# One more wait ahead of the experts' first weight loads into the ring, in a two-layer hybrid trunk with a routed mixture of experts

## What is computed

```python
def moe(h, router_w, router_bias, w_gate, w_up, w_down):      # 16 experts, width 1024 -> 256 -> 1024
    ...
        scores = jax.nn.sigmoid((xb @ router_w).astype(jnp.float32))
        sel = scores + router_bias
        ...
        # best group of 4 experts by its two best, then the top 2 experts inside it
        combine = jnp.sum(jax.nn.one_hot(e_idx, N_EXPERTS, dtype=jnp.float32) * wts[..., None], 1)
        hid = jax.nn.silu(jnp.einsum('td,edf->tef', xb, w_gate)) * jnp.einsum('td,edf->tef', xb, w_up)
        return jnp.einsum('tef,te,efd->td', hid, combine.astype(hid.dtype), w_down)
```

## Time and profile before

| what | value |
|---|---|
| median of the runs | 1359.54 us |
| the profiled execution | 1359.39 us |
| its span, first to last instruction | 1357.6 us |
| PE, DVE, ACT, POOL busy | 75%, 39%, 21%, 6% |
| DMA: all data, mean rate | 239.50 MB, 176 GB/s |
| mean granted TensorE clock | 0.849 |

### The profile page before, as it was taken

The page is one execution under the profiler, slowest core; times in us unless marked ns, Lnnn a source line. Parts: engine busy times, 40 slices in busy tenths (PEclk is TensorE's granted clock), DMA queues, the critical chain, the costliest instruction groups (busy, mean ns, idle before and its releaser), DMA issues. The chain is left out here.

```text
span 1357.6 us, 23829 instructions
## 1 busy us (share of the span) xinstructions
PE 1021.0 (75%) x10191; PEld 703.7 (52%) x10191; DVE 532.0 (39%) x1335; ACT 286.3 (21%) x610; POOL 85.6 (6%) x144
## 2 busy tenths in 40 slices
PE   4999768399758888875499967849857975987651
PEld 3556556388435675532355646539734564553321
DVE  0255462956562331111415554486574142111103
ACT  1210344322410211100121044432240030110000
POOL 0000000000000012211100000000000002221111
PEclk8999868789978868999699977769977967998775
DMA  9596313400116179997732231240014119999933
GB/s 387 208 261 213 125 63 125 186 5 8 63 54 260 62 281 359 357 380 256 261 114 94 96 122 63 88 162 4 8 63 170 51 38 388 329 363 371 378 102 140
DMA packets 39443, 239.50 MB, mean 176 GB/s; under 512 B 5344, under 2 KB 5344, under 8 KB 15776
## 3 DMA queue, kind: packets, MB, share of 16 engines
q1 hardware_dynamic: 26784, 194.56, 38.2%
q0 software_dynamic: 12544, 43.27, 10.1%
HBM read 210.02 MB, written 27.79 MB: 175 GB/s over the span
## 5 line engine op out<-in xcount | busy, mean ns | idle before, releaser
L836 PE MATMUL bank<-sb_hT,sb_ring 128*128 128x385 f32 (+1 forms) x640 | 211.0, 490 | 5.0 <-ACT sb_hT L1378 5.0
L836 PE MATMUL bank<-sb_arena 64*64 64x64 f32 (+6 forms) x1184 | 139.6, 326 | 42.9 <-DVE sb_arena L1630 24.0
L836 PEld LDWEIGHTS bank<-sb_hT,sb_ring 128*128 128x128 f32 (+1 forms) x640 | 119.2, 188 | 93.8 <-issue 12.3
L1378 ACT ACTIVATE sb_arena<-bank 128x384 f32<-128x384 f32 (+5 forms) x166 | 69.9, 442 | 368.3 <-PE bank L836 266.5
L836 PEld LDWEIGHTS bank<-sb_arena 128*64 128x64 f32 (+2 forms) x1184 | 87.4, 150 | 74.1 <-DVE sb_arena L1630 25.3
L839 PE MATMUL bank<-sb_consts,sb_arena 64*128 64x64 f32 (+1 forms) x451 | 62.9, 289 | 57.4 <-DMA sb_arena<-x_slots 28.7
L1378 ACT ACTIVATE sb_u<-bank 128x256 f32<-128x256 f32 (+2 forms) x92 | 41.7, 463 | 261.3 <-PE bank L836 260.6
L836 PE MATMUL bank<-sb_ring,sb_arena 128*64 128x256 f32 (+1 forms) x536 | 86.4, 474 | 11.4 <-DMA sb_ring<-weights 8.3
L836 PE MATMUL bank<-sb_o,sb_ring 128*128 128x385 f32 x256 | 86.9, 502 | 9.5 <-issue 9.5
L839 PEld LDWEIGHTS bank<-sb_consts,sb_arena 64*128 64x128 f32 (+1 forms) x451 | 50.4, 165 | 80.4 <-issue 76.2
L1630 DVE TENSOR_TENSOR sb_arena<-sb_arena,bank 128x128 f32<-128x128 f32 (+1 forms) x91 | 26.0, 320 | 162.6 <-ACT sb_arena L1378 148.2
(11 more groups left out here) (174 smaller groups left out, 1252.9 us busy)
## 6 DMA issues: line engine op xcount, KB each, us to landing
sb_ring<-weights SPq DMA_DIRECT2D x117, 1024.0 KB, 8.6
sb_u<-weights SPq DMA_DIRECT2D x24, 1024.0 KB, 16.7
sb_arena<-weights SPq DMA_DIRECT2D x24, 1024.0 KB, 20.9
sb_arena<-x_slots POOLq DMA_DIRECT2D x35, 256.0 KB, 7.6
y_slots<-sb_arena POOLq DMA_DIRECT2D x70, 128.0 KB, 6.8
sb_sq<-weights SPq DMA_DIRECT2D x8, 1024.0 KB, 20.2
sb_hT<-weights SPq DMA_DIRECT2D x8, 1024.0 KB, 20.3
x_slots<-sb_arena POOLq DMA_DIRECT2D x1, 6912.0 KB, 40.2
```

Of the source, the lines that this page charges most:

```text
L836: return nc.tensor.matmul(out, lhsT, rhs, start=start, stop=stop, skip_group_check=True)
L1378: return nc.scalar.activation(out, in_, func, **kw)
```

## The change

Per layer, the first load of an expert's item into the ring gets one wait ahead of it: SP waits until `scattered` shows that all six scatters of this layer have landed, as POOL does at L788.

```diff
+            first_late = [min(n for n, (where, _) in enumerate(stream)
+                              if where[:2] == ("expert", l) and HOMES[home[n]][0] == "ring") for l in range(DEPTH)]
             for m, n in enumerate(load_order):
                 where = stream[n][0]
                 kind, l = where[:2]
...
                         sp.dma_start(small[:, :], a["small"][l + 1]).then_inc(small_loaded, 16)
+                    if b < EXPERTS and n == first_late[l]:
+                        sp.wait_ge(scattered, 6 * 16 * (l + 1))
                     if b < EXPERTS:
                         load_item(l, n, a["weights"][l * LAYER_ITEMS + DENSE_ITEMS + b * EXPERT_ITEMS + j])
```

## The result

The changed kernel takes 1375.83 us (median of 6 runs, 1374.83 to 1382.53) against 1359.19 us before (6 runs). The ratio is 1.0122, 95% interval 1.0098 to 1.0146. The profiled execution took 1375.93 us, its span 1374.1 us, 16.5 us over the span before.

What follows compares the result with a forecast made beforehand. The prediction took DMA time left unused before each expert stage's saturated stretch to bound the kernel. It summed 1359.4 us + 10.7 (layer 0) + 9.4 (layer 1) to 1379.5 us, 1.5% slower, range 1368 to 1388 us.

Steps and rivals of the forecast that it cites:

- The bound: In both expert stages, DMA time left unused before the saturated stretch decides; DMA is full from 510 to 630 us in layer 0.
- The sum: Whole kernel: 1359.4 us plus 10.7 for layer 0 and 9.4 for layer 1 gives 1379.5 us, 1.5% slower.
- The scatters' time: In each layer, the six scatters running alone take 12.4 us, as the gathers at layer 1's end did.
- The hole: At each expert stage's start, held ring loads clear 12.2 and 11.0 us later; less idle won back, 10.7 and 9.4 us.
- What is gained counts for nothing: At block 2, scatters landing 2.8 and 4.2 us sooner restart PE sooner, but it then waits longer at the DMA limit.
- the fetch taking "what it did": At block 2, fetching token rows takes as long as before, ring loads beside it standing in for u and arena loads.
- rival A: In both expert stages token rows are the limit, so PE's earlier restart reaches the end: 1352.4 us; chance 0.07.
- What is late next: At block 3, first to use ring items, no stall in layer 0: items there at 514 us, needed at 524 us.
- B: In both layers the scatters land no sooner, adding 2.8 + 4.2 us: 1386.5 us; chance 0.10.
- C: Through the expert stages, earlier freed homes refill the queue faster, giving back half of 20.1 us: 1369.5 us; chance 0.10.
- D: At SP's wait in each layer, the wait is already over, so no effect within the measurement: about 1360 us; chance 0.07.
- The two rates and the rule: Five ring loads take 12.5 us at 421 GB/s; at 358 GB/s each layer is 2.1 us worse; rule: issue DMAs early.

Runs made afterwards that it cites:

- quarter loads: Kernel before and changed kernel, each loading only a quarter of the columns of expert items behind a layer's first thirteen: 1289.73 and 1289.28 us.
- second trace: The changed kernel measured and profiled again with nothing altered, beside the kernel before on one chip: 1380.71 against 1364.51 us, ratio 1.0124.
- e3_until_rows: Against the changed kernel, SP waits only until DVE has the tokens' slots, not until the scatters land; ratio to the kernel before 1.0159.
- e1_layer0_only: Against the changed kernel, the wait for the scatters stands in layer 0 only; ratio to the kernel before 1.0057.

## Why the prediction was right, step by step

**The bound.** Right: DMA time ahead of the saturated stretch decides. The quarter loads show it: the same wait, 16.6 us with the limit and none without.

**The sum.** Forecast 20.1 us, measured 16.6: the mechanism held, and the size was 3.5 us too large. The scatters' time, below, is 3.0 us of it. The kernels with the wait in one layer measured 7.8 us for layer 0 and 8.7 us for layer 1, where 10.7 and 9.4 us were forecast.

**The hole.** In single executions, against the forecast 10.7 and 9.4 us, the stages show 11.3 and 7.3 (again 11.4 and 7.6 us in the second trace, against the same trace of before). Two of its terms were off, in opposite directions. The scatters alone took 10.9 us to SP's release (497.56 to 508.42 us), not the 12.4 us that the gathers of the earlier trace rows gave. And the start of the scatters after hT's load, taken as fixed, is not: in layer 1 it was 9.5 us in the trace of before and 12.3 us in the changed kernel's. By these two layer 1 should have cost 9.4 - 1.5 + 2.8 = 10.7 us; it cost 7.3. Layer 0 by the same reckoning (start 12.7 and 12.4 us) should have cost 10.7 - 1.5 - 0.3 = 8.9 us; it cost 11.3. So the near hit of 10.7 us in layer 0 is partly luck, and the misses of the two layers nearly cancel. For layer 1 there is a part of an answer. The share of the windows above fell from 0.78 to 0.70, 10.4 us of the 130, but the data was only 9.0 us late, so the engines moved more for each busy microsecond (254 GB/s at 0.70 against 279 at 0.78). Why they did, and where the last 1.7 us went, is open.

**What is gained counts for nothing.** Right in effect: PE went on behind the token rows 31.9 us after hT's load instead of 35.6 (517.04 - 485.13, and 517.18 - 481.58), and its waits for weights grew by more. My reason for the fetch taking "what it did" was sound in the full kernel (8.35 us against 7.77) and in the quarter form, where it took 3.2 us more, is the reason why hardly any gain was left for rival A.

**What is late next.** Right: no stall at block 3; the first wait for weights came at 546.35 and 1186.81 us, forecast 550 and 1190. The next layer's first load left at 668.89 us, forecast 664.7; 3.6 us of that lay ahead of the stage. One thing the forecast did not look at: behind the full stretch of layer 1, from 1288 us before and from about 1304 us after, the DMA share is 0.34 and 0.37, and PE waits three times for token rows of the last blocks, 14.2 us before and 14.8 after. The end of that stage is not bound by DMA. It takes nearly as long in both (38.0 and 39.4 us from the first of these waits' end to the first gather), so the lateness passes through it.

**The rivals.** A (token rows are the limit) is out: the rows came sooner and the kernel is slower, and without the DMA limit it is even. B (scatters land no sooner) is out: 11.1 us alone until POOL goes on, 15.2 beside the old backlog, 28.6 when the loads start with them. C (half given back, 10 us) is out: 16.6 us stayed. D (no effect) is out. What none of them said is that the loads beside the scatters can cost more than the wait, as in `e3_until_rows`: the point of protecting the scatters is real, but the kernel before had most of it already (15.2 us of a possible 11.1 to 28.6), since its ring loads went out 12 us ahead of them.

**The two rates and the rule.** The sum by the 421 GB/s of the earlier trace rows gave 20.1 us and was 3.5 us too large. The Trainium skill, "DMA: Bandwidth & Descriptors", section Specifications, gives an HBM limit per core of about 358 GB/s; by it the sum would have been an estimated 24.3 us. The measured 16.6 us lie nearer to the row. That a DMA is to be issued early and waited on late (the Trainium skill, "DMA: Bandwidth & Descriptors", Rules for kernel authors) agrees with both ends here: 16.6 us lost by holding five loads back, some 8 us won by sending them ahead of hT's.

## What to carry to other kernels

In a stage that the DMA engines limit, look at how many bytes they have moved by the time they are full: what is missing then came out at the end here within 2.5 us, however long the other engines' waits inside looked. Where bulk loads disturb a small transfer that others wait for, try sending them earlier than it before holding them back; if their buffers seem to forbid it, see what stands ahead of them in the queue. And ask of a wait that protects a transfer what else its semaphore releases at the same moment.

## What the runs showed of the hardware that I had not expected

The start of the scatters jumps between about 9.6 and 12 us after hT's load, in either layer and with or without the change. It goes with TensorE's granted clock in the 18 matmuls that count the tokens. In 6 of the 24 stages of the twelve traces they take 2.15 us at a granted clock of 1.00, which is 2.4 GHz, and the scatters start 9.5 or 9.6 us after hT's load. In the other 18 they take 3.61 to 3.99 us at 0.50 to 0.56, mostly the level of 1.2 GHz, and the scatters start 11.7 to 12.7 us after it. First `e1_layer0_only`, then the full change, layer 0, each with the window of these matmuls:

```profile
484.71 2.15 PE L840 MATMUL bank<-sb_arena,sb_consts 128*128 128x16 f32 x18 [1.53 <-DVE sb_arena L1634]
...
484.71:486.86 2.15, 2.15 (x22) 2.12 (x26) 0.00 (x0) 0.00 (x0) 0.00 (x0) 1.00 0.89 351
```

```profile
487.61 3.99 PE L840 MATMUL bank<-sb_arena,sb_consts 128*128 128x16 f32 x18 [2.51 <-DVE sb_arena L1634]
...
487.61:491.60 3.99, 3.99 (x22) 3.95 (x26) 0.00 (x0) 0.00 (x0) 0.00 (x0) 0.50 0.39 164
```

The 24 transposes just before are the other way round. In the six they take 5.36 us, all at 0.50, and the clock rises behind them. In the other 18 they take 4.13 to 4.71 us: the clock rises among them, to 0.91 to 1.00 in their last microsecond, PE then waits 2.2 to 2.8 us for DVE, and the count runs at the low level again. What decides between the two isn't shown. The matmuls themselves account for 1.5 to 1.8 us of the difference; the rest of the 2 to 3 us lies in the waits around them. With the wait for the scatters in place, this start sets how long the DMA engines stand idle.
